# Two decoder layers on one core: small moves at the start, in the mixing stage, in the gates and in the last product

## What is computed

```
x += 0.5 * swiglu(rms_norm(x, g1), w1, w3, w2)
h  = rms_norm(x, gm) @ w_in          # a_u, a_v, q, k, v, c_q, gates
y_a = gelu(a_u) * spatial_gate(layer_norm(gelu(a_v)))
y_b = block_sparse_attention(rope(q), rope(k), v, paged old keys and values)
y_c = cross_attention(c_q, memory keys, memory values)
g_a, g_b, g_c = split(sigmoid(gates))
x += (g_a * (y_a @ w_a) + g_b * (y_b @ w_b) + g_c * (y_c @ w_c)) @ w_o
x += 0.5 * swiglu(rms_norm(x, g2), v1, v3, v2)
```

## Time and profile before

| what | value |
|---|---|
| median of 3 runs | 1528.53 us (1528.47 to 1528.87) |
| the profiled execution | 1527.0 us |
| its span, first to last instruction | 1525.3 us |
| instructions | 28869 |
| DVE busy | 897.7 us (59%) |
| ACT busy | 705.5 us (46%) |
| mean granted clock of TensorE | 0.995 |
| moved by transfers | 316.03 MB, 207 GB/s on average |

### The profile page before, as it was taken

How to read it: one execution, slowest core, us unless ns; L and a number is a source line. 1 busy time by engine, 2 the same in 40 slices (tenths; PEclk the granted TensorE clock), 3 DMA queues, 4 the chain that set the end, 5 groups by cost and what they waited for, 6 DMA issues and landing times. The chain is left out here.

```text
span 1525.3 us, 28869 instructions
## 1 busy us (share of the span) xinstructions
PE 1492.3 (98%) x12100; PEld 1440.4 (94%) x12100; DVE 897.7 (59%) x1207; ACT 705.5 (46%) x938; POOL 103.9 (7%) x198
## 2 busy tenths in 40 slices
PE   7999999999999999999999999999999999999996
PEld 7999999998878999999999999999988889999995
DVE  6676446656744775555565654665656537655543
ACT  6544335446643454443444443544565435544342
POOL 0000001140012000000000000023100210000000
PEclk9999999999999999999999999999999999999998
DMA  6555659794698544455555466688856955444551
GB/s 241 183 180 190 190 173 322 259 358 155 215 342 292 168 159 165 163 165 162 170 166 176 166 201 181 222 288 301 314 194 208 357 190 199 159 165 162 159 165 66
DMA packets 107026, 316.03 MB, mean 207 GB/s; under 512 B 13392, under 2 KB 13392, under 8 KB 106768
## 3 DMA queue, kind: packets, MB, share of 16 engines
q1 hardware_dynamic: 94320, 273.67, 54.0%
q0 software_dynamic: 12576, 40.51, 7.3%
HBM read 306.00 MB, written 5.77 MB: 204 GB/s over the span
## 5 line engine op out<-in xcount | busy, mean ns | idle before, releaser
L1158 DVE TENSOR_TENSOR wlo<-wraw,whi 128x1024 fp32r<-128x1024 f32 (+2 forms) x447 | 511.0, 1148 | 516.6 <-ACT whi L831 514.9
L476 PE MATMUL res<-norm_hi,whi 128*128 128x288 f32 x2176 | 652.1, 300 | 13.6 <-DVE wlo L1151 7.9
L476 PE MATMUL res<-norm_lo,whi 128*128 128x288 f32 x2176 | 643.3, 296 | 0.0
L831 ACT ACTIVATE whi<-wraw 128x1024 fp32r<-128x1024 f32 (+2 forms) x447 | 441.3, 993 | 433.5 <-PE res L476 361.6
L476 PE MATMUL res<-norm_hi,wlo 128*128 128x288 f32 x2176 | 641.2, 295 | 0.0
L476 PEld LDWEIGHTS res<-norm_hi,whi 128*128 128x128 f32 x2176 | 409.1, 188 | 25.4 <-issue 8.8
L476 PEld LDWEIGHTS res<-norm_hi,wlo 128*128 128x128 f32 x2176 | 411.0, 189 | 0.0
L476 PEld LDWEIGHTS res<-norm_lo,whi 128*128 128x128 f32 x2176 | 410.0, 188 | 0.5
L476 PE MATMUL res<-h_hi,whi 128*128 128x288 f32 x1024 | 304.3, 297 | 1.3 <-DVE h_lo L1597 0.8
L476 PE MATMUL res<-h_lo,whi 128*128 128x288 f32 x1024 | 302.1, 295 | 0.0
L476 PE MATMUL res<-h_hi,wlo 128*128 128x288 f32 x1024 | 301.3, 294 | 0.0
(11 more groups left out here) (221 smaller groups left out, 1096.7 us busy)
## 6 DMA issues: line engine op xcount, KB each, us to landing
wraw<-in_ffn_w SPq DMA_DIRECT2D x240, 512.0 KB, 3.5
wraw<-in_w_in SPq DMA_DIRECT2D x96, 512.0 KB, 5.6
wraw<-in_ffn_w SPq DMA_DIRECT2D x32, 384.0 KB, 3.3
page_Q<-in_cache_k POOLq DMA_DIRECT2D x48, 256.0 KB, 6.0
page_Q<-in_cache_k SPq DMA_DIRECT2D x40, 256.0 KB, 5.8
page_Q<-in_cache_v SPq DMA_DIRECT2D x40, 256.0 KB, 5.2
wraw<-in_w_mem_kv SPq DMA_DIRECT2D x16, 512.0 KB, 3.4
page_Q<-in_cache_v POOLq DMA_DIRECT2D x32, 256.0 KB, 6.8
```

The lines of the kernel that those rows point to most:

```text
L476: mm = pe.matmul(res[:, 2 * s + c, 0:n], w_, m_, start=begin and k == 0 and j == 0, stop=end and k == kh - 1 and j == 2)
L831: act.activation(whi[n % NH][:, 0:kh, :], wraw[n % NR][:, 0:kh, :], ACT.Copy).then_inc(hi_done, 1)
L1158: dve.tensor_tensor(wlo[n % NR][:, 0:kh, :], wraw[n % NR][:, 0:kh, :], whi[n % NH][:, 0:kh, :].bitcast(F32), ALU.subtract).then_inc(lo_don ...
```

## The change

The first unit comes in two loads with semaphores of their own, and the gains are issued by ACT. In the mixing stage part a of the probabilities is turned behind half unit 20 instead of 18, b right behind it, n behind 21, in other banks, and ACT empties them later. In the gates ACT's turn n empties the probabilities of head n-2 behind the unit of step n-1 and ahead of the exponentials, where before it ended with those of head n-1. DVE copies the memory results ahead of scores, products and conversions. The 32-row operands become 128 rows, filled with zeros by POOL. DVE makes all of the last product.

More of the change, by code:

```diff
@@ L214, in layer @@
         u += [("kS0", 0), ("vr0", 2), ("vr1", 3), ("kS1", 1),
-              ("vr2", 2), ("rep", 3), ("newS", 2), ("kS2", 0), ("ln1", 3), ("pTa0", 2), ("ln2", 3), ("pTb0", 2),
-              ("kS3", 1), ("pTn0", 2), ("vn0", 2), ("vn1", 3), ("vn2", 2), ("sgu0", 3), ("sgu1", 2), ("sgu2", 3),
+              ("vr2", 2), ("rep", 3), ("newS", 2), ("kS2", 0), ("ln1", 3), ("ln2", 3), ("pTa0", 2), ("pTb0", 3),
+              ("pTn0", 1), ("kS3", 1), ("vn0", 2), ("vn1", 3), ("vn2", 2), ("sgu0", 3), ("sgu1", 2), ("sgu2", 3),
               ("sgu3", 2)]
@@ L368, in build @@
     raw_loaded = [sem(f"raw_loaded{u}") for u in range(NR)]
-    first_hi, first_lo = sem("first_unit_hi"), sem("first_unit_lo")
+    first_raw, first_hi, first_lo = sem("first_unit_raw"), sem("first_unit_hi"), sem("first_unit_lo")
     hi_done, lo_done, w_used = sem("hi_done"), sem("lo_done"), sem("w_used")
@@ L382, in build @@
     kz_zero, ke_ready, ko_ready = sem("k_head_zeros"), sem("k_even_ready"), sem("k_odd_ready")
-    ones_ready = sem("ones_ready")
+    ones_ready, ra_zero = sem("ones_ready"), sem("new_rows_zero")
     q_shifted, k_shifted = sem("q_shifted"), sem("k_shifted")
-    xg_ready, rstd_final, y_pool = sem("x_gain_ready"), sem("rstd_final"), sem("y_pool_ready")
+    xg_ready = sem("x_gain_ready")
     p_max, p_exp, p_nrm = sem("row_max"), sem("probs_exp"), sem("probs_normal")
@@ L1192, in inverse_deviation @@
             to, std = (mrstd, mrstd) if name == "memsum.0" else (rstd, sqs)
[L1193 to L1196, removed]
-            else:
-                step(i)
+            step(dve.reciprocal(to[:], std[:]))
         def ffn(L, f, u0, gain):
@@ L1573, in gates @@
                     step(dve.reciprocal(col(70, 2), col(68, 2)))
[L1574 to L1577, removed]
-                    dve.tensor_copy(cq[:, :, SEQ + 16 * h:SEQ + 16 * h + 16].rearrange("p c (b t) -> p c b t", b=4),
-                                    own_heads(nm)[:, :, :, 0:4]).then_inc(emptied_of(nm), 1)
                 if n == 15:
@@ L1717, in _ @@
         for g in range(4):
-            if g == 2:
-                sp.wait_ge(y_pool, 1)
-            else:
-                sp.wait_ge(nf_ready, 4 * DEPTH + min(g, 2) + 1)
+            sp.wait_ge(nf_ready, 4 * DEPTH + g + 1)
             sp.dma_start(A["y"][:, 2 * g:2 * g + 2, :], yout[:, 2 * g:2 * g + 2, :]).then_inc(out_y, 16)
```

## The result

The changed kernel takes 1508.04 us in the median of five, and in a second set of runs 1507.11. Its ratio to the kernel before is 0.9865, 95% interval [0.9853, 0.9877], and in the second set 0.9861 [0.9846, 0.9876]: 20.6 and 21.2 us of 1528.5 less, where 13.7 were forecast. The profile shown is one of the second set, since that of the first fell into a disturbed run (2429.6 us, at a mean granted clock of 0.557). The one shown took 1507.98 with a span of 1506.3, against 1527.0 and 1525.3 before. So 19.0 us are to be found between two traces, and the page's first row gives only 4.4 of it to a shorter busy time of PE.

A forecast was written before the change was run, and what follows sets the result against it. PE, busy for 98% of the span, was taken as the bound. Terms of 0.5 + 0.85 + 4.8 + 1.3 + 1.05 + 1.4 + 3.3 + 0.5 = 13.7 us off 1528.53 gave 1514.8, range 1511.5 to 1522.0.

The forecast's parts named there:

- Last product: End of the kernel: DVE makes all four products, POOL's leaves the path; 0.5 us won (0.3 to 0.8).
- Gates: Unit results emptied ahead of turned probabilities, sigmoid's table load running early: 2.4 us per layer, 4.8 in all (3.0 to 5.6).
- first rival: Table load still in the way or a small wait replacing a removed one: 1519.0, or 1521.5 with low tiles; chance 0.2.
- Clock: Layer 1 behind the sigmoid wait: granted clock averages 0.65; without the wait 1.3 us come back (0 at the other end).
- Low halves: Branch a: PE's wait for low halves goes as ACT makes high halves sooner; 1.05 us won (0 to 1.05).
- copies: Memory results copied into cq by DVE ahead of a product and two conversions: 0.69 us twice, 1.4 (0.9 to 1.4).
- Tiles: Full-size operands for 32-row products: 2.5 us from small products, 0.8 from 512-column ones; 3.3 together (0.8 to 3.9).
- Mixing stage: Old-key probabilities turned two units later: 0.85 us won in all (0 to 1.6), layer 1 giving its 0.83 back.
- second rival: No change that shows: stretches hanging on DMA give PE's lead back; 1524.2, or 1527.5 without tiles; chance 0.05.
- the forecast wait for the sample's rows: Sign of a right forecast: in layer 1's mixing stage, PE's wait for these rows grows to about 1 us.
- Start: Before the first scaling: first unit in two loads, gains on ACT's queue; 0.5 us won (0 to 1.0).
- turned probabilities behind conversions: Rival in the gates: ACT's copy stands behind DMA-bound weight conversions, making the kernel slower, 1533.6; chance 0.04.

The follow-up runs named there:

- The end alone: Kernel before with only the last product's third unit pair moved from POOL to DVE, nothing left for POOL at the end: 1518.96 us, ratio 0.9947.
- the product that nobody needs: Changed kernel with POOL also multiplying two chunks of a dead tile at the place of its old product: 1514.02 us, ratio 0.9910.
- the fill: Changed kernel with POOL filling two chunks of a dead tile with zeros at the place of its old product: 1511.87 us, ratio 0.9896.
- the earlier product: Changed kernel with POOL multiplying two chunks of a dead tile some 50 us before the end, nothing after: 1506.67 us, ratio 0.9863.

## Why the prediction was wrong, point by point

**Last product: the step that failed.** It said 0.5 (0.3 to 0.8); it was 6.5. The step priced DVE's four products, which won the 0.5, and let what lies behind them stand as it was; it said that POOL's product leaves the path entirely, meaning the product's own 1.9. What leaves is the drain behind it, 5.4 of the 6.5. The mechanism (POOL off the end) was right, the size wrong, since I ended my reading with the chain of waits, which stops at 1516.57 in a span of 1525.3 (the 98% of PE in the earlier trace rows hides that). The 8.7 between were never asked for: stores need 2.9 of them (the last landed at 1519.45), the barrier the rest. A row of that line did stand in the chain: the 1.87 on line 1805, which the step reads as DVE's second product, is DVE's closing drain; the product took 1.95. The end alone, the product that nobody needs, the fill and the earlier product show this. The low end of the range was mis-added, too: its five terms make 2.95 and not 3.3, so 1511.9; both measured times lie below either.

**Gates** held: 4.87 against 4.8. The table load did run ahead of PE's result, so the first rival falls in its main form. In the trace the sigmoid starts 0.02 behind the load's end (354.62 and 1.28, then 355.92), so the further drain of 1.38 us in the Trainium skill (ScalarE: Activation LUTs, What ACT_TABLE_LOAD costs) did not appear here either.

**Clock** held in size, 1.5 against 1.3, for the two profiled executions. That it was one layer's was this execution's chance: with 8 falls in six profiles at 1.5 each, the kernel before loses 2.0 an execution on average, by estimate.

**Low halves and copies** held, 1.05 and 1.4; but the copies needed no move of their own, since the gates alone remove that wait, too. The sum counted it once, so it was not hurt by that. **Tiles** came to 2.4 (alone 2.7) of 3.3: six records won 0.29 for 0.32, but layer 1 took 0.55 back in one of its two steps, where PE now waits 0.2 for DVE before the spatial gate; the rest of that is open. The Trainium skill (TensorEngine Tiling, When to Use Tiling) recommends row tiles for a contraction of 32, and the edit that gave them up gained; 0, as by that rule, lies outside its interval.

**Mixing stage** was to give layer 1's share back, because landings would not move when PE did, while layer 0 had the room. The first half of this was wrong. ACT's conversion in layer 1 of the changed kernel:

```profile
1085.64 1.06 ACT L833 ACTIVATE whi<-wraw 128x1024 fp32r<-128x1024 f32 x1 [5.77 <-DMA wraw<-in_w_in]
```

It waits 5.77 for the same load, but the load landed 6.32 us sooner, as far as PE was ahead in this stretch (6.4). The loads are issued on PE's progress, as the second rival itself had it; here an earlier PE moved the load. In layer 0 of the same trace the load did not come sooner, though PE was 0.8 ahead: the conversion starts at 342.43, and before at 342.46. PE still did not wait there, and the layers kept 0.8 and 0.9. In the trace with the product that nobody needs that conversion started at 343.71, and PE waited:

```profile
343.71 1.06 ACT L833 ACTIVATE whi<-wraw 128x1024 fp32r<-128x1024 f32 x1 [6.31 <-DMA wraw<-in_w_in]
```

```profile
345.55 0.68 PE L651 MATMUL gb<-sgu_wT,rows_a 128*128 128x128 f32 x4 [0.74 <-ACT rows_a L976]
```

So the forecast wait for the sample's rows exists, but not where it was put and not of its size: over the seven traces with this edit it is 0.2 and 0.7 in layer 0 of two, 0.3 in layer 1 of two others, and none in three. That the two traces compared above show 1.7 is in part luck; it lies a little over the upper end of 1.6.

**Start** gave nothing between these two traces: PE's lead of 1.4 at the first product was gone at the 97th, where the first scaling makes it wait. That is the luck of an early execution of the kernel before; over all traces it is about 1.0, the upper bound of its 0.5.

**The rivals** of no change and of turned probabilities behind conversions are not borne out: no wait of PE for probabilities exists, and a stretch that hangs on DMA gave back little: 0.7 at most of the waits above.

## What to carry to other kernels

Read the span to its last microsecond: if the chain of waits ends before the span does, ask for the instructions of the closing line and what SP waits for there. POOL's closing record can hold the end after late work, even where nobody needs the result, so give late helper work to the engines already at the end, or have POOL done early enough (here some 10 us before the last store lands, an estimate from its 9.7). Before calling a load unmoved, ask what issues it: one issued on the bottleneck's progress can move with the bottleneck, as one did here in layer 1 and did not in layer 0. Before adding up parts that were measured alone, look in their traces for a wait that two of them remove. And before a difference between two traces is called a term, see how far the same stretch differs between executions.

## What the runs showed of the hardware

POOL's closing drain ended 9.71 to 9.73 us behind the end of its last piece of work in all fourteen traces: behind a product of 1.9 us (1515.3 to 1525.0, and 1503.1 to 1512.9), one of 1.4 (1432.15 to 1441.9), a fill of 0.6 (1503.3 to 1513.0) and a DMA issue (1219.6 to 1229.3). DVE and ACT have no such tail: their closing drains end within 0.06 us of their last work (DVE's in the changed kernel, 1500.9 and 2.8, at 1503.7). What POOL does in these 9.7 us stays open. And a stop of PE of 2.5 us was followed by a fall of its granted clock to the lower level in 8 of 12 cases, and by none in 4.
